# Two FFNs with gate and up products of 512 columns over both operand parts

## The reference, cut to what matters

```python
f = conv_ffn(rms_norm(h, norm_ffn[i]), ffn_w_gate[i], ffn_conv_w[i], ffn_conv_b[i], ffn_w_up[i], ffn_w_down[i])
h = h + f
# conv_ffn: g = x @ w_gate (1024 -> 2816), a causal convolution of 3 taps over the tokens of g plus a bias,
#           gelu(conv(g)) * (x @ w_up) @ w_down (2816 -> 1024)
# rms_norm: x * rsqrt(mean(x * x) + eps) * gain
```

## Time and profile before

| | us |
|---|---|
| median of 3 runs (1115.63 to 1117.27) | 1117.15 |
| the profiled execution's own time | 1117.09 |
| its span, first to last instruction | 1115.3 |
| TensorE matmuls busy | 1076.9 (97%) |
| VectorE busy | 721.8 (65%) |
| ScalarE busy | 593.4 (53%) |
| GpSimd busy | 141.1 (13%) |

### The profile page before, as it was taken

One profiled execution on the slowest core, in us unless ns is written; L12 is line 12 of the kernel. 1 busy time (PEld: TensorE's weight loads), 2 busy tenths in 40 slices (PEclk: granted clock), 3 DMA queues, 4 the chain that ended last, 5 costly groups with the idle time before them and its releaser, 6 DMA issues.

```text
span 1115.3 us, 19860 instructions
## 1 busy us (share of the span) xinstructions
PE 1076.9 (97%) x8074; PEld 954.2 (86%) x8074; DVE 721.8 (65%) x1222; ACT 593.4 (53%) x981; POOL 141.1 (13%) x165
## 2 busy tenths in 40 slices
PE   8999999999999999898999999999999999999998
PEld 6777888655878898598989999999987799999997
DVE  4565656386454767876775686676776666676674
ACT  4452666545244666665565664454573545454454
POOL 0000010253020000614331100000014311000000
PEclk9999999999999999998999999999999999999999
DMA  9732211277413332054543455555543243645551
GB/s 385 292 114 76 77 68 46 98 280 249 169 38 112 119 135 100 1 189 136 200 152 120 151 189 189 196 182 190 175 166 113 78 135 131 217 162 189 198 193 44
DMA packets 25242, 168.77 MB, mean 151 GB/s; under 512 B 3264, under 2 KB 3264, under 8 KB 5312
## 3 DMA queue, kind: packets, MB, share of 16 engines
q1 hardware_dynamic: 23616, 165.41, 42.1%
q10 hardware_dynamic: 1536, 2.10, 0.6%
HBM read 164.35 MB, written 1.05 MB: 148 GB/s over the span
## 4 chain that ended last, share of the span: by engine, by line
PE 84%; DVE 5%; ACT 5%; issue 2%; POOL 1%; DMA 1%; ACTq 0%; SPq 0%; DVEq 0%; POOLq 0%
PE bank L421 24%; PE bank L423 23%; PE bank L422 23%; DVE wlo L415 2%; ACT whi L400 2%; PE bank L1382 2%; PE bank L1516 2%; PE bank L467 1%; PE bank L1526 1%; PE bank L1536 1%; DMA PROJ<-in_stream 1%; PE bank L1409 1%; PE bank L1400 1%; PE bank L1255 1%; ACT TILE L1569 1%
## 5 line engine op out<-in xcount | busy, mean ns | idle before, releaser
L421 PE MATMUL bank<-OPH,whi 128*128 128x256 f32 (+1 forms) x1700 | 518.2, 305 | 4.9 <-ACT AV L2769 2.7
L423 PE MATMUL bank<-OPH,wlo 128*128 128x256 f32 (+1 forms) x1700 | 509.6, 300 | 0.0
L422 PE MATMUL bank<-OPL,whi 128*128 128x256 f32 (+1 forms) x1700 | 509.6, 300 | 0.0
L415 DVE TENSOR_TENSOR wlo<-raw,whi 128x1024 fp32r<-128x1024 f32 (+1 forms) x256 | 305.7, 1236 | 108.6 <-ACT whi L400 108.3
L421 PEld LDWEIGHTS bank<-OPH,whi 128*128 128x128 f32 x1700 | 326.2, 192 | 23.7 <-issue 6.2
L422 PEld LDWEIGHTS bank<-OPL,whi 128*128 128x128 f32 x1700 | 326.3, 192 | 10.7 <-issue 1.2
L423 PEld LDWEIGHTS bank<-OPH,wlo 128*128 128x128 f32 x1700 | 326.2, 192 | 10.3
L400 ACT ACTIVATE whi<-raw 128x1024 fp32r<-128x1024 f32 (+1 forms) x256 | 255.9, 1050 | 88.3 <-PE bank L423 88.3
L421 PE MATMUL bank<-whi,OPH 128*128 128x256 f32 (+2 forms) x272 | 93.7, 344 | 5.0 <-DVE OPL L632 3.6
L422 PE MATMUL bank<-wlo,OPH 128*128 128x256 f32 (+2 forms) x272 | 91.1, 335 | 0.0
L423 PE MATMUL bank<-whi,OPL 128*128 128x256 f32 (+2 forms) x272 | 91.0, 335 | 0.0
(11 more groups left out here) (281 smaller groups left out, 1150.7 us busy)
## 6 DMA issues: line engine op xcount, KB each, us to landing
raw<-in_stream SPq DMA_DIRECT2D x143, 1024.0 KB, 4.9
PROJ<-in_stream SPq DMA_DIRECT2D x5, 1024.0 KB, 18.8
raw<-in_stream SPq DMA_DIRECT2D x4, 1056.0 KB, 10.0
PROJ<-PROJ ACTq DMA_DIRECT2D x32, 64.0 KB, 3.8
FIRST<-in_first SPq DMA_DIRECT2D x1, 1248.0 KB, 5.9
C<-in_con SPq DMA_DIRECT2D x1, 1157.5 KB, 7.9
FIRST<-in_first SPq DMA_DIRECT2D x1, 1024.0 KB, 7.9
out<-PROJ SPq DMA_DIRECT2D x4, 256.0 KB, 2.1
```

Of the source, the lines that this page charges most:

```text
L415: nc.vector.tensor_tensor(c.w[1][:, part], c.raw[:, part], c.w[0][:, part].bitcast(F32), ALU.subtract).then_inc(*raises(c.lo[h]))
L421: nc.tensor.matmul(out, w[0], x[0], start=start, stop=False, skip_group_check=skip)
L422: nc.tensor.matmul(out, w[0], x[1], start=False, stop=False, skip_group_check=skip)
L423: return nc.tensor.matmul(out, w[1], x[0], start=False, stop=stop, skip_group_check=skip)
```

## The change

Gate and up chunks now take two banks each, one for each half t: gates always banks 0 and 1, ups always 2 and 3. `OPH` and `OPL` become two halves of one tensor `OP`, so that one matmul with whi can stream both, 512 columns, into a whole bank; the matmul with wlo adds its 256 columns to the first half of the bank. What was three matmuls is two. The two halves of a bank have to be added: VectorE's product by the factor becomes a reduction over pairs. The factor is multiplied by GpSimd, in place, for gates and for ups. The splits of two chunks move within the programs of ScalarE and VectorE. Down products stay as they are.

```diff
-        OPH, OPL = sb("OPH", [P, KD, T], F32R), sb("OPL", [P, KD, T], F32R)
+        OP = sb("OP", [P, 2, KD, T], F32R)
+        OPH, OPL = OP[:, 0], OP[:, 1]
...
+        def products_apart(out, w, x, start, stop):
+
+            nc.tensor.matmul(out, w[0], x, start=start, stop=False, skip_group_check=True)
+            return nc.tensor.matmul(out[:, 0:SEQ], w[1], x[:, 0], start=False, stop=stop, skip_group_check=True)
...
             for c in range(NF):
-                g.append(GBANK.take("pe", ("dve",)))
-                up.append(GBANK.take("pe", ("dve",)))
+                for made, at in ((g, 0), (up, 2)):
+                    made.append([b.take("pe", ("dve",)) for b in banks[at:at + 2]])
+                    made[c][0].freed[:] = made[c][1].freed
...
-                by["gate", c].used, by["up", c].used = g[c].full, up[c].full
+                t2.append(tile.take("pool", ("act", "dve")))
+                by["gate", c].used, by["up", c].used = g[c][1].full, up[c][1].full
...
+            def halves(made):
+                bank = twin[0] if made is g else twin[1]
+                return bank[:].rearrange("p t (h n) -> p t n h", h=2)
+
+            def both(k):
+                return OP[:, :, k, lo:lo + SEQ]
+
+            def wide(e, us, ch):
+                for point in due(e, [u.empty for u in us], ch.lo):
+                    e.wait_ge(*point)
+                for t, u in enumerate(us):
                     for k in range(KD):
                         for point in due(e, op_block(k)):
                             e.wait_ge(*point)
-                        mm = products(u.mem[:, t * SEQ:(t + 1) * SEQ], cols(ch, k, t * P, P), op(k, lo, SEQ), k == 0,
-                                      k == KD - 1)
-                mm.then_inc(*raises(u.full))
+                        mm = products_apart(u.mem, cols(ch, k, t * P, P), both(k), k == 0, k == KD - 1)
+                mm.then_inc(*raises(us[1].full))
...
-                both = [(g[0], by["gate", 0]), (up[0], by["up", 0])]
+                opening = [(g[0], by["gate", 0]), (up[0], by["up", 0])]
                 for k in range(KD):
-                    for u, ch in both:
-                        for point in due(e, u.empty, ch.lo[k // 4], op_block(k)):
+                    for us, ch in opening:
+                        for point in due(e, [u.empty for u in us], ch.lo[k // 4], op_block(k)):
                             e.wait_ge(*point)
-                        for t in range(2):
-                            mm = products(u.mem[:, t * SEQ:(t + 1) * SEQ], cols(ch, k, t * P, P), op(k, lo, SEQ),
-                                          k == 0 and t == 0, k == KD - 1, skip=True)
+                        for t, u in enumerate(us):
+                            mm = products_apart(u.mem, cols(ch, k, t * P, P), both(k), k == 0, k == KD - 1)
                         if k == KD - 1:
-                            mm.then_inc(*raises(u.full))
+                            mm.then_inc(*raises(us[1].full))
                 total.add(e)
...
                     split_hi(e, by["gate", c].s + (3 if c else 4))
+                    split_hi(e, by["up", c].s + 3)
...
-                    split_hi(e, by["up", c].s + 3)
                     e.wait_ge(*when(("conv_done", l, c)))
                     nc.scalar.activation(t1[c].mem[:], t1[c].mem[:], ACT.Gelu).then_inc(*raises(("gelu_made", l, c)))
-                    for point in due(e, t2[c].full):
+                    if c < NF - 1:
+                        split_hi(e, by["up", c].s + 4)
+                    for point in due(e, ("hidden_made", l, c)):
                         e.wait_ge(*point)
...
                     split_lo(e, by["gate", c].s + (3 if c else 4))
-                    for point in due(e, g[c].full, ("factor_made", f"ffn{l}"), ("pads_zeroed", l, c % 2)):
+                    for point in due(e, g[c][1].full, ("pads_zeroed", l, c % 2)):
                         e.wait_ge(*point)
                     if c >= 2:
                         for point in due(e, ("newest_tap", l, c - 2), ("conv_done", l, c - 2)):
                             e.wait_ge(*point)
-                    nc.vector.tensor_tensor(pad[c % 2][:, :, 2:SEQ + 2], two(g[c].mem), rr, ALU.mult).then_inc(*raises(("gate_scaled", l, c)))
+                    nc.vector.tensor_reduce(pad[c % 2][:, :, 2:SEQ + 2], halves(g), AXX, ALU.add).then_inc(
+                        *raises(g[c][1].read["dve"]))
+                    split_lo(e, by["up", c].s + 3)
...
-                    split_lo(e, by["up", c].s + 3)
-                    for point in due(e, up[c].full, t2[c].empty):
-                        e.wait_ge(*point)
-                    nc.vector.tensor_tensor(two(t2[c].mem), two(up[c].mem), rr, ALU.mult).then_inc(*raises(up[c].read["dve"]))
-                    for point in due(e, ("gelu_made", l, c), up[c].read["dve"]):
-                        e.wait_ge(*point)
-                    nc.vector.tensor_tensor(t2[c].mem[:], t1[c].mem[:], t2[c].mem[:], ALU.mult).then_inc(*raises(t2[c].full))
+                    for point in due(e, up[c][1].full, t2[c].empty):
+                        e.wait_ge(*point)
+                    nc.vector.tensor_reduce(two(t2[c].mem), halves(up), AXX, ALU.add).then_inc(*raises(up[c][1].read["dve"]))
+                    if c < NF - 1:
+                        split_lo(e, by["up", c].s + 4)
+                    for point in due(e, ("gelu_made", l, c), t2[c].full):
+                        e.wait_ge(*point)
+                    nc.vector.tensor_tensor(t2[c].mem[:], t1[c].mem[:], t2[c].mem[:], ALU.mult).then_inc(
+                        *raises(("hidden_made", l, c)))
...
+            def pool(e):
+                total.pool(e)
+                for c in range(NF):
+                    for point in due(e, g[c][1].read["dve"], ("factor_made", f"ffn{l}")):
+                        e.wait_ge(*point)
+                    x = pad[c % 2][:, :, 2:SEQ + 2]
+                    nc.gpsimd.tensor_tensor(x, x, rr, ALU.mult).then_inc(*raises(("gate_scaled", l, c)))
+                    for point in due(e, up[c][1].read["dve"]):
+                        e.wait_ge(*point)
+                    nc.gpsimd.tensor_tensor(two(t2[c].mem), two(t2[c].mem), rr, ALU.mult).then_inc(*raises(t2[c].full))
...
-                g[c].freed[:] = [("gate_scaled", l, c)]
-                t1[c].freed[:] = [t2[c].full]
+                t1[c].freed[:] = [("hidden_made", l, c)]
```

More of the change, by code:

```diff
@@ L2593, in ffn @@
             rr = r.unsqueeze(1).broadcast_to([P, 2, SEQ])
-            def wide(e, u, ch):
-                for point in due(e, u.empty, ch.lo):
+            def halves(made):
[5 more added lines that the diff above has]
+                for point in due(e, [u.empty for u in us], ch.lo):
                     e.wait_ge(*point)
-                for t in range(2):
+                for t, u in enumerate(us):
                     for k in range(KD):
```

5 lines of the change are left out of this document (2 added, 3 removed).

## The result

The changed kernel takes 1130.45 us (median of 4 runs, 1127.13 to 1131.52) against 1117.13 on the same chip: a ratio of 1.0123, 95% interval 1.0109 to 1.0137. The profiled execution took 1130.09 us (span 1128.2). Slower was right; the size was not: +13.3 us where I had forecast +4.8, just outside my range.

The account below looks back on a forecast made before the run. TensorE, whose matmuls never stop in an FFN, was taken as the bound. Terms -8.7 + 1.7 + 7.8 + 1.2 + 2.8 = +4.8 us on 1117.09 gave 1121.9 us; range 1117.5 to 1130.

Parts of the forecast that it names:

- wide product: Gate and up products: three 256-column matmuls (0.3597 us) become one of 512 and one of 256 (0.3474); 704 save 8.7 us.
- opening waits for banks: Each FFN's opening: gate 0 needs both banks, so waits for the preceding stage's last eviction; together 1.7 us.
- gate 1 waits for gate 0: After each opening: gate 1 waits for VectorE's reduction of gate 0, 3.9 us, twice: 7.8 us.
- small waits, last down: Each FFN: 0.5 us at the last down product, plus 0.2 at c = 1 and 2; 1.2 us in all.
- clock behind the openings: After each opening's 3.9 us idle time the clock falls to 1.2 GHz for 3.4 us; 2.8 us in all.
- rival 1: Behind the openings the clock stays at 2.4 GHz: +2.0, 1119.1 us; chance 0.17.
- the turns that GpSimd and VectorE take: Steady part: running together they slow each other; two GpSimd products take 3.50 us instead of 2.6.
- VectorE's round: Steady part: VectorE needs 16.4 us a round against TensorE's 16.9 and 16.6, winning back only 0.2 to 0.6 each c.
- third: Gate and up pairs: a 256-column matmul behind 512 costs its columns alone, 0.333 us a pair; -5.2, 1111.9 us; chance 0.10.
- The second: Steady part: VectorE's round outgrows TensorE's, lateness reaches the last down, 4.2 more an FFN; +10.4, 1127.5 us; chance 0.23.

Follow-up runs that it names:

- three-product kernel: Changed kernel with each pair's 512-column matmul put back as two of 256 columns; ratio 1.0166 to the kernel before.
- factor on VectorE: Changed kernel with both multiplications by the norm factor on VectorE, right behind their reductions, instead of GpSimd; ratio 1.0108 to the kernel before.
- table last: Changed kernel, but behind the FFNs ScalarE makes the upper part of the next stage's second chunk before loading its table; ratio 1.011 to the kernel before.
- shifted kernel: Kernel before the change with 8 matmuls of 128 columns on constants ahead of gate 1 of the first FFN; ratio 1.002 to the kernel before.
- grouped: Changed kernel, but behind the opening each half's eight 512-column matmuls stand together, then its eight of 256, instead of taking turns; ratio 1.0109 to the kernel before.

## Why the prediction was right in sign and wrong in size

| step | forecast us | measured us |
|---|---|---|
| wide product | -8.7 | -4.4 (704 x 0.0063) |
| opening waits for banks | +1.7 | +1.7 |
| gate 1 waits for gate 0 | +7.8 | +8.1 (2 x (4.30 - 0.24)) |
| small waits, last down | +1.2 | +0.5 |
| clock behind the openings | +2.8 | +3.0 to 3.2 |
| wait behind the first FFN | 0 | +2.3 |
| clock in the middle stage | 0 | +1.7 (one more stretch in this execution) |
| sum | +4.8 | +12.9 to 13.1 (last matmul: +12.9) |

The measured column is read from one profiled execution of each kernel and from the experiments' profiles.

**The gain failed by half.** The step that failed is "It becomes one of 512 and one of 256, 0.3474 us". I priced a pair as the sum of two spacings, each read among equals. One round ran at that price, nearly all others at 0.353 to 0.354. My rows couldn't show that, and my bounds had it (0.333 to 0.36), but I took the sum as if it were measured. The three-product kernel shows the worth of what is left, 0.4%. Why most pairs take the longer spacing stays open: it is not the two pieces of the operand, and not the turns alone.

The Trainium skill's 2.5 ns a matmul ("TensorE: Matmul & The Clock Gate", section "Wait — 56ns, not 53.3ns?") would have given 1.8 us, an estimate from that page; the measured 4.4 lie between it and my rows.

**VectorE at the end of the FFN.** The step that failed is "With what lateness is left I put 0.5 us at the last down in each FFN". It stops at that product and puts the stage behind it at nothing, and there TensorE waited 2.3 us. Nor was it lateness left from the opening. VectorE was on time for the last gate:

```profile
797.45 1.22 DVE L2722 TENSOR_REDUCE PROJ<-bank 128x512 f32<-128x1024 f32 x1 [1.16 <-PE bank L429]
```

From there to the end of h's lower part at 808.61 it takes 11.2 us, as I had counted (11.4). Before, the same chain took 8.7 (794.02 to 802.73). The extra 2.5 us pass on to what stands behind on VectorE, the two splits and then the sums. The kernel that reduces gate 0 first still waits 1.79 us there, the one with the shorter chain (factor on VectorE) 0.76, the one with the table last 0.72.

**The clock.** The falls behind the openings came as forecast, shown by filling the wait. That a wait of 1.77 us in the middle stage can have one I had excluded without saying so, from the one execution in which it hadn't. The wait of 1.55 us that I cited for rival 1, as one without a fall, had a fall in the next execution that was profiled. The shifted kernel shows that such a fall can come with the old FFNs too; how many the change adds in the mean stays open. My length for a fall was also read from too narrow a window: around 520 us the clock was low for 6.8 us, from 519.4 on, and not for the 3.6 of the earlier trace rows:

```profile
519.40:526.20 6.80, 5.56 (x26) 5.56 (x27) 5.79 (x9) 3.42 (x6) 3.50 (x2) 0.50 0.47 170
```

Behind the openings of the changed kernel it was 3.4 us, as I had put it; in the profiles of the grouped and the table-last kernels the first opening is followed by 6.8.

**Right:** both waits for banks, to 0.3 us, with their releasers; VectorE's 1.22 us for a reduction (forecast 1.21); and the turns that GpSimd and VectorE take. VectorE's round fitted with more room than I gave it:

```profile
647.42 1.22 DVE L2722 TENSOR_REDUCE PROJ<-bank 128x512 f32<-128x1024 f32 x1
663.15 1.22 DVE L2722 TENSOR_REDUCE PROJ<-bank 128x512 f32<-128x1024 f32 x1
...
695.04 1.22 DVE L2722 TENSOR_REDUCE PROJ<-bank 128x512 f32<-128x1024 f32 x1 [0.36 <-PE bank L429]
```

A late round takes 15.73 us, not 16.4, and wins back 1.3 us against TensorE's 17.07, so VectorE is on time at c = 4 in the first FFN (c = 2 in the second), where I had expected it near 9. The Trainium skill's warning ("Perfetto Trace Analysis", section "Optimizing Scalar/DVE Operations") holds stronger than I used it: the kernel without GpSimd's part has VectorE less busy and 1.4 us less wait behind the first FFN.

Rivals: the first and third did not come. The second gives 1127.5 us, closer to the result than my forecast, but for a cause that isn't there: VectorE's round did not outgrow TensorE's. Its sum is also wrong: 4.8 and twice 4.2 are +13.2, 1130.3 us, and not +10.4. That would have met the result by luck.

## What to carry to other kernels

A spacing read among equals need not be the spacing in a mixed series, so carry it as a bound and not as a measurement: here it held for one round of the first FFN and missed by 6 ns a pair in the rest. When a chain on another engine gets longer, follow that engine's queue past the place where this is harmless, to the first thing behind it that the bounding engine needs; and when a bank gets shared, ask first what stands before its reader at the one place where there is no slack: here one moved split was worth 5.6 of 13 us. A few us of difference between two single profiles can be one or two falls of the clock at a place the change never touched: count the stretches before explaining them, and in more than one execution before calling them caused.

## What the runs showed of the hardware

- Starts of float32r matmuls, each with its own weight load, at the full clock: 512 columns behind 512 after 0.2275 us (down products before) or 0.231 (groups of eight), 256 behind 256 after 0.120 or 0.119. A pair of 512 and 256 in turn took 0.3534 us in most rounds and 0.3469 in one, in groups of eight 0.3491. One or two pieces of operand, 2 or 16 KB apart, made no difference to the 0.3534.
- A matmul of 128 columns on plain float32 constants, two rows in the trace, takes 0.22 us.
- The same 1.77 us wait was followed by no half clock (before, and before with 16 extra matmuls), by 3.4 us (with 8) and by 6.8 us (changed kernel), in one execution each. A 1.55 us wait was followed by none (before) and by 3.4 us (changed kernel). Each 3.4 us behind an opening cost about 1.5 us.
- A GpSimd product that runs while VectorE splits weights gets between its instructions: 1.30 us become 2.10 to 2.20, and a pair of splits 3.35 instead of 2.36.
